# Two-layer mixer and MoE trunk: value block first, weights of the next layer loaded earlier, and half of the first projection ahead of the second tile's norm

## What is computed

```python
z = x @ w_in                                   # 1024 -> 6656 columns: qa ka va ub qc kc vc ga gb gc
merged = sigmoid(ga) * (ya @ w_branch_a) + sigmoid(gb) * (yb @ w_branch_b) + sigmoid(gc) * (yc @ w_branch_c)
x = layer_norm(alpha * x + merged @ w_out, ln1_g, ln1_b)
y = shared_expert(x) + routed_experts(x)       # 64 experts, 8 of them for each token
x = layer_norm(alpha * x + y, ln2_g, ln2_b)    # then the next layer
```

## Time and profile before

| | us |
|---|---|
| median of 3 executions | 1582.39 |
| lowest, highest | 1580.69, 1586.14 |
| the profiled execution | 1581.64 |
| its span | 1579.8 |

### The profile page before, as it was taken

One profiled execution on the slowest core, in us unless ns is written; L12 is line 12 of the kernel. 1 busy time (PEld: TensorE's weight loads), 2 busy tenths in 40 slices (PEclk: granted clock), 3 DMA queues, 4 the chain that ended last, 5 costly groups with the idle time before them and its releaser, 6 DMA issues.

```text
span 1579.8 us, 21900 instructions
## 1 busy us (share of the span) xinstructions
PE 1525.8 (97%) x8898; PEld 948.7 (60%) x8898; DVE 565.5 (36%) x1009; ACT 414.4 (26%) x655; POOL 34.5 (2%) x30
## 2 busy tenths in 40 slices
PE   7999999999999999999789999999999999999996
PEld 7899996444454444445388999864444444544542
DVE  4567735222222222222545577351222222212224
ACT  4545422121111112112235544221111211211111
POOL 0101000000000000000001110000000000000000
PEclk9999999999999999999989999999999999999998
DMA  8543458799999999699733544587999999996991
GB/s 292 175 170 138 153 206 374 288 426 424 415 421 414 405 417 414 244 414 419 282 107 107 187 161 160 210 331 317 426 425 416 419 401 416 419 411 249 415 412 75
DMA packets 79741, 495.86 MB, mean 314 GB/s; under 512 B 6080, under 2 KB 11456, under 8 KB 46656
## 3 DMA queue, kind: packets, MB, share of 16 engines
q1 hardware_dynamic: 77392, 491.31, 76.9%
q10 hardware_dynamic: 2288, 3.67, 0.7%
HBM read 493.92 MB, written 1.05 MB: 313 GB/s over the span
## 4 chain that ended last, share of the span: by engine, by line
PE 94%; DVE 2%; DMA 2%; ACT 1%; issue 1%; SPq 0%; DVEq 0%
PE bank L1406 28%; PE bank L1252 19%; PE bank L1432 14%; PE bank L1361 8%; PE bank L1378 8%; PE bank L1322 4%; PE bank L1209 3%; PE bank L1191 2%; DMA ring_w<-in_w_in 2%; PE bank L1418 1%; PE bank L1393 1%; PE bank L1369 1%; ACT w_hi L594 1%; PE bank L1264 1%; PE bank L1290 1%
## 5 line engine op out<-in xcount | busy, mean ns | idle before, releaser
L1252 PE MATMUL bank<-x_hi,w_hi 128*128 128x256 f32 x688 | 198.4, 288 | 3.5 <-ACT arena L646 1.9
L1252 PE MATMUL bank<-x_lo,w_hi 128*128 128x256 f32 x688 | 195.4, 284 | 0.0
L1252 PE MATMUL bank<-x_hi,w_lo 128*128 128x256 f32 x688 | 195.3, 284 | 0.0
L1126 DVE SCALAR_TENSOR_TENSOR hid<-hid,gate_s,bank 128x256 f32<-128x256 f32 x64 | 30.8, 481 | 399.7 <-ACT hid L707 399.7
L1406 PE MATMUL bank<-arena 128*64 128x512 f32 x768 | 170.1, 595 | 0.0
L1406 PE MATMUL bank<-gu_a,arena 128*64 128x512 f32 x768 | 170.1, 595 | 0.0
L1140 DVE TENSOR_TENSOR y_lo<-bank,y_hi 128x512 fp32r<-128x512 f32 x128 | 88.6, 692 | 225.3 <-ACT y_hi L713 225.3
L777 DVE TENSOR_TENSOR w_lo<-ring_w,w_hi 128x2048 fp32r<-128x2048 f32 x63 | 143.9, 2288 | 66.3 <-ACT w_hi L594 66.2
L1361 PE MATMUL bank<-onehot,xg_hi 128*128 128x256 f32 x512 | 139.9, 306 | 4.0 <-DVE onehot L946 4.0
L713 ACT CAST y_hi<-bank 128x512 fp32r<-128x512 f32 x128 | 74.9, 585 | 246.1 <-PE bank L1432 246.1
L1252 PEld LDWEIGHTS bank<-x_hi,w_hi 128*128 128x128 f32 x688 | 132.7, 193 | 7.5 <-issue 4.0
(11 more groups left out here) (186 smaller groups left out, 1996.4 us busy)
## 6 DMA issues: line engine op xcount, KB each, us to landing
gu_a<-in_expert_w_gate_up SPq DMA_DIRECT2D x24, 4096.0 KB, 13.7
arena<-in_expert_w_gate_up SPq DMA_DIRECT2D x24, 4096.0 KB, 14.6
ring_w<-in_expert_w_gate_up SPq DMA_DIRECT2D x32, 2048.0 KB, 10.9
ring_w<-in_w_in SPq DMA_DIRECT2D x25, 2048.0 KB, 8.6
dn_a<-in_expert_w_down SPq DMA_DIRECT2D x24, 2048.0 KB, 12.1
arena<-in_expert_w_down SPq DMA_DIRECT2D x24, 2048.0 KB, 11.2
dn_c<-in_expert_w_down SPq DMA_DIRECT2D x16, 2048.0 KB, 11.7
ring_w<-in_w_out SPq DMA_DIRECT2D x4, 2048.0 KB, 7.9
```

The source lines that it names most:

```text
L1252: ins = mm(b[:, S * c:S * c + S], lhs, rhs, start=(k == 0 and a + w == 0), stop=(k == KD - 1 and a == 1))
```

## The change

1. The value block `va` is the first of the z blocks, so z tasks 0 and 1 are of the kind that multiplies x (stationary, by token tile) with weights (moving). The attention tasks in `plan()` move by one z task, `rope` of kc stands after z task 10 and `pv` 3 after z task 11.
2. `first_tile(l, u, t)`: z tasks 0 and 1 are done by token tile. In layer 1, PE does the half of tile 0 of z task 0 behind `xt` (0, 1), and that of z task 1 behind `xt` (0, 3); the halves of tile 1 follow as the z tasks. In layer 0 both tiles are done at their task, with the low weights last, and the first low part is cut along k instead of the columns.
3. The second norm of layer 0 is cut in `norm_stats` and `norm_apply`. DVE makes `x_lo` of tile 0 between the statistics and the application of tile 1, and ACT makes `x_hi` of tile 0 ahead of the root of tile 1.
4. SP issues the first two blocks of layer 1 when pair 23 has done its up projection, not after the last expert load.
5. ACT makes the high parts of chunks 0 and 1 behind the SiLU of the last but one pair, that of chunk 2 at the start of the last pair; DVE makes the three low parts between the two pair steps.
6. The low part of z task 19's chunk is made ahead of the reciprocals of `rms` (0, 0).
7. `scores` 0 and 1 each wait for the two z tasks that they read, not for four.

```diff
-Z_BLOCKS = [("qa", 0), ("ka", 512), ("va", 1024), ("qc", 2048), ...
+Z_BLOCKS = [("va", 1024), ("qa", 0), ("ka", 512), ("qc", 2048), ...
-        4: sc(0), 5: sc(1), 6: tr(0) + sc(2), 7: [("pv", 0, 0)] + tr(1) + sc(3),
-        8: [("pv", 1, 0)] + tr(2) + [("rope", 0, 0), ("rope", 0, 1)], 9: [("pv", 2, 0)] + tr(3),
-        10: [("pv", 3, 0), ("rope", 1, 0), ("rope", 1, 1)], 11: sc(4), 12: sc(5), 13: tr(4) + sc(6),
+        5: sc(0), 6: sc(1), 7: tr(0) + sc(2), 8: [("pv", 0, 0)] + tr(1) + sc(3),
+        9: [("pv", 1, 0)] + tr(2) + [("rope", 0, 0), ("rope", 0, 1)],
+        10: [("pv", 2, 0)] + tr(3) + [("rope", 1, 0), ("rope", 1, 1)],
+        11: [("pv", 3, 0)] + sc(4), 12: sc(5), 13: tr(4) + sc(6),
...
-        at[inside[0] if inside else PLAN[last]] = n
+        long = [PLAN[k] for k in range(first, last + 1) if PLAN[k] == ("rms", 0, 0)]
+        at[inside[0] if inside else long[0] if long else PLAN[last]] = n
...
-                for n in range(NB - 2):
+                for n in range(0 if l == 0 else 2, NB - 2):
                     load_block(l, n)
...
+                if l + 1 < L:
+                    sp.wait_ge(up_done, 2 * start + SHORT_FROM - 2)
+                    for n in range(2):
+                        load_block(l + 1, n)
...
-                    if last and l + 1 < L:
-                        for u in range(WBUFS):
-                            split_high(l + 1, u)
+                    if last and odd and l + 1 < L:
+                        split_high(l + 1, 2)
                     act.wait_ge(up_done, n + 1)
                     nc.scalar.activation(hid[:], bank_up[:, 0:FE], ACT.Silu).then_inc(silu_ready, 1)
+                    if last and not odd and l + 1 < L:
+                        split_high(l + 1, 0)
+                        split_high(l + 1, 1)
...
-                for t in range(TT):
-                    norm_std(act, l, 1, t)
+                norm_std(act, l, 1, 0)
+                if l + 1 < L:
+                    for j in range(2):
+                        x_high(l + 1, j)
+                norm_std(act, l, 1, 1)
...
+                    if kind == "rms" and task in LOW_AT:
+                        split_low(l, LOW_AT[task])
...
-                    pair_step(n, u, n - l, last=u == 1)
-                norm(l, 1)
+                    pair_step(n, u, n - l)
+                    if u == 0 and l + 1 < L:
+                        for c in range(WBUFS):
+                            split_low(l + 1, c)
+                norm_stats(l, 1, 0)
+                norm_apply(l, 1, 0)
+                norm_stats(l, 1, 1)
+                if l + 1 < L:
+                    for j in range(2):
+                        x_low(l + 1, j)
+                norm_apply(l, 1, 1)
...
+            def first_tile(l, u, t):
+                n = CHUNK_AT["z", 0, u]
+                tokens = slice(P * t, P * t + P)
+                b = bank(l, ("z", u, 0))
+                pe.wait_ge(w_hi_ready, NC * l + n + 1)
+                for a, w in ((0, 0), (0, 1), (1, 0)) if l else ((0, 0), (1, 0), (0, 1)):
+                    if a:
+                        for g in (2 * t, 2 * t + 1):
+                            wait_evac(pe, l, ("xt", 0, g))
+                    else:
+                        pe.wait_ge(x_hi_ready, 4 * l + 2 * t + 2)
+                    for k in range(KD):
+                        if w and (l, u) == (0, 0) and k == 0:
+                            pe.wait_ge(first_low_ready, 1)
+                        if w and k == (KW if (l, u) == (0, 0) else 0):
+                            pe.wait_ge(w_lo_ready, NC * l + n + 1)
+                        ins = mm(b[:, S * t:S * t + S], (x_hi, x_lo)[a][:, k, tokens], chunk_part((w_hi, w_lo)[w], n)[:, k, :],
+                                 start=(k == 0 and a + w == 0), stop=(k == KD - 1 and (w if l == 0 else a) == 1))
+                return ins
...
+                    elif kind == "z" and i < 2:
+                        for t in range(TT) if l == 0 else (1,):
+                            ins = first_tile(l, i, t)
...
+                    if l and task in (("xt", 0, 1), ("xt", 0, 3)):
+                        u = j // 2
+                        acquire(l, ("z", u, 0))
+                        first_tile(l, u, 0)
```

More of the change, by code:

```diff
@@ L594, in split_high, with x_high @@
                 nc.scalar.copy(chunk_part(w_hi, n), chunk_in(n)).then_inc(w_hi_ready, 1)
+            def x_high(l, j):
+                task = ("xt", 0, j)
+                wait_task(act, l, task)
+                nc.scalar.copy(x_tile(x_hi, j),
+                               bank(l, task)[:].rearrange("p (c n) -> p c n", c=4)).then_inc(x_hi_ready, 1)
             start = 0
@@ L604, in _ @@
                     if kind == "xt" and i == 0:
-                        wait_task(act, l, task)
-                        nc.scalar.copy(x_tile(x_hi, j), b[:].rearrange("p (c n) -> p c n", c=4)).then_inc(x_hi_ready, 1)
+                        if l == 0 or j >= 2:
+                            x_high(l, j)
                         if l == 0 and j == 3:
@@ L729, in _ @@
                 start = start + more * HALVES + HALVES
-                pair_step(2 * start - 2, 0)
+                pair_step(2 * start - 2, 0, last=True)
                 pair_step(2 * start - 1, 1, last=True)
@@ L769, in first_low @@
                 for c in range(2):
-                    cols = slice(P * c, P * c + P)
-                    v.tensor_tensor(lo[:, :, cols], full[:, :, cols], hi[:, :, cols].bitcast(F32),
+                    ks = slice(KW * c, KW * c + KW)
+                    v.tensor_tensor(lo[:, ks, :], full[:, ks, :], hi[:, ks, :].bitcast(F32),
                                     ALU.subtract).then_inc((first_low_ready, w_lo_ready)[c], 1)
@@ L799, in lambdas, with x_low, norm_stats @@
                     step(v.tensor_scalar(nlam[:, l:l + 1], nlam[:, l:l + 1], -lambda_init[l], None, ALU.add))
[L801 to L805, removed]
+            def x_low(l, j):
+                task = ("xt", 0, j)
+                dve.wait_ge(x_hi_ready, 4 * l + j + 1)
+                free(v.tensor_tensor(x_tile(x_lo, j), bank(l, task)[:].rearrange("p (c n) -> p c n", c=4),
+                                     x_tile(x_hi, j).bitcast(F32), ALU.subtract), l, task)
+            def norm_stats(l, which, t):
+                    k = 2 * l + which
                     row = x_tok[:, t, :]
@@ L818, in norm, with norm_apply @@
                     v.bn_aggr(mean_var[:, t, :], stats[:].rearrange("p a b -> p (a b)")).then_inc(var_ready, 1)
+            def norm_apply(l, which, t):
+                    k = 2 * l + which
+                    row = x_tok[:, t, :]
+                    dve.wait_ge(ln_in, 32 * (k + 1))
                     dve.wait_ge(var_ready, TT * k + t + 1)
@@ L960, in _ @@
                     pair = b[:].rearrange("p (c n) -> p c n", c=2)
+                    if kind == "rms" and task in LOW_AT:
+                        split_low(l, LOW_AT[task])
                     if kind == "xt" and i == 0:
-                        dve.wait_ge(x_hi_ready, 4 * l + j + 1)
-                        free(v.tensor_tensor(x_tile(x_lo, j), b[:].rearrange("p (c n) -> p c n", c=4),
-                                             x_tile(x_hi, j).bitcast(F32), ALU.subtract), l, task)
+                        if l == 0 or j >= 2:
+                            x_low(l, j)
                         if (l, j) == (0, 3):
@@ L1081, in _ @@
                                         ALU.subtract).then_inc(y_lo_ready_of[n], 1)
-                    if kind != "scores" and task in LOW_AT:
+                    if kind not in ("scores", "rms") and task in LOW_AT:
                         split_low(l, LOW_AT[task])
@@ L1090, in _ @@
                     if task == ("branch", 2, 3):
-                        norm(l, 0)
+                        for t in range(TT):
+                            norm_stats(l, 0, t)
+                            norm_apply(l, 0, t)
                     if task == ("router", 0, 0):
@@ L1103, in _, with pair_step @@
                         later_rounds(l)
-                def pair_step(n, odd, combined_before, following=None, last=False):
+                def pair_step(n, odd, combined_before, following=None):
                     bank_up, bank_other = (bank_even, bank_odd)[::-1 if odd else 1]
@@ L1222, in _ @@
                             ins = nc.tensor.transpose(b[:, P * c:P * c + P], x_tok[:, t, 4 * (j % 2) + c::KD], ident)
+                    elif kind == "z" and i < 2:
+                        for t in range(TT) if l == 0 else (1,):
+                            ins = first_tile(l, i, t)
                     elif kind == "z":
-                        if i == 0:
-                            for g in range(4):
-                                wait_evac(pe, l, ("xt", 0, g))
                         n = CHUNK_AT["z", i // 2, i % 2]
                         hi, lo = chunk_part(w_hi, n), chunk_part(w_lo, n)
[L1229 to L1240, removed]
```

(6 more changed lines are left out.)

7 lines of the change are left out of this document (1 added, 6 removed).

## The result

The changed kernel takes 1568.84 us (median of 4 executions, 1567.74 to 1570.28) beside 1582.98 us for the kernel before: a ratio of 0.9912, 95% interval 0.9900 to 0.9924. It was run twice more with the kernel before beside it, and gave 0.9921 (0.9908 to 0.9935) and 0.9919 (0.9906 to 0.9933). The forecast was 1572.9 us with a range of 1569.5 to 1578.5. The median of all 14 executions of the changed kernel is 1569.4 us, at the range's lower end.

A forecast was written before the change was run, and what follows sets the result against it. PE, busy 97% of the span, was taken as the bound; gains of 1.6 + 4.6 + 3.3 = 9.5 us took the profiled 1581.64 to 1572.1, plus 0.75 for the median: 1572.9 us, range 1569.5 to 1578.5.

The forecast's parts named there:

- Last pair: Last pair of layer 0: with blocks loaded early, the product starts sooner after the up projection; gain 1.6 us, bounds 1.0 and 2.1.
- Transfer: Expert stage, pair 23: two weight blocks fit a hole in DMA, in by 664 us; price 0, at worst 10.8 us.
- Between the layers: From the second norm to z task 1 of layer 1: early half tiles gain 4.6 us, bounds 1.4 and 5.8.
- The price on the second norm: Between the layers: making two `x_lo` first delays the second tile's `ln_done` by 1.2 us.
- Low part ahead of the reciprocals: Mixer, ahead of `branch` (1, 0): the wait goes, gain 1.9 us in each layer before the new task order's price.
- The price for the new order of tasks: Mixer, after z task 10: the second `rope` may wait; 0.25 us a layer taken, 0.7 at most.
- the first step: Whole kernel: PE is busy 97% of the span, so time can come only from its gaps or low-clock matmuls.
- The estimate by the Trainium skill: Low clock between the layers: throttled time times share taken away gives 2.8 us more, sum 12.3; not used in the forecast.
- B: Between the layers or mixer: the clock or a new wait takes most of a term, 1576.1 or 1576.2 us; chance 0.22.
- C: Between the layers: no slow matmul, gain 5.8 us; with other terms at their bounds 11.7, time 1570.7 us; chance 0.08.
- D: Expert stage: the 4.2 MB load does not fit the hole at pair 23; slower, 1583.7 to 1588.4 us; chance 0.04.
- E: Half tiles do not start early and the mixer's new wait eats its gain; 1578.5 to 1581 us; chance 0.04.

The follow-up runs named there:

- the filled pair: The kernel before and the changed kernel, each with matmuls on constants put in PE's idle places: medians 1575.97 and 1567.13 us.
- the filled kernel: The changed kernel with matmuls on constants into free banks in four idle places of PE: ratio to the kernel before 0.9900, median 1567.13 us.

## Why the prediction was right and wrong

**Last pair: right.** 1.6 us in the sum, 1.8 in the profile. The fit of ACT's two casts into 3.98 us held, and DVE is what is late now, as said. What the step left out is that behind PE's stop of 2.1 us there the clock fell in three of four profiles: it is the place at 774.

**Transfer: right**, price 0, in by 662 for a forecast of 664.

**Between the layers: right in mechanism, 0.6 us short.** 4.6 forecast, 5.2 in the profile. 14 matmuls of the half tile started at half clock and not 18, 0.4 us; the other 0.2 is in the time before, where the sum ended z task 1 at 810.6 and the profile at 810.84. The second turning ran at the full clock (0.90 us), as the sum took it. The price on the second norm was 1.0 us, forecast 1.2. The sum took the early halves as the whole gain; the run without them has 1.4 of it. There z tasks by token tile do not wait for the last `x_lo`, and fewer of their matmuls meet the low clock.

**Low part ahead of the reciprocals: right.** 3.8 us forecast before its price, gaps of 1.88 from start to start gone in both layers, alone, and back when it was taken back. The price for the new order of tasks, forecast at 0.25 us a layer at the second `rope` of z task 10, was 0.25 as idle time of PE and 0.4 from start to start. The mixer of layer 1 gained 1.6 us, forecast 1.65.

**What failed** is the first step: "So time can come only from PE's gaps, or from matmuls at a low clock; the change removes no matmul." The sentence names the low clock, and the working then looked for it between the layers alone. Everywhere else it was taken that a stretch that is not edited stays as long as it is. The kernel before had two low stretches at the gathering, 1.7 us each, that a table by stretch would have shown, and a third place at 774 in which it may fall. None of the sum's terms holds them, and the changed kernel has lost them and has one at 74 instead. Why the falls went there no run shows; taking part 6 alone back brought the one at 283 again. The balance in the two profiles is 3.4 - 1.6 = 1.8 us. Over all executions the filled pair puts the clock's part at 4 us, of which the sum had about 1 (the second turning at the full clock). The bounds were made from the terms, and had no room for it. A second, smaller step failed beside it: 0.75 us were added to get from the profiled execution to the median. The profiled execution of the changed kernel came out 12.4 us lower and not 9.5, and its median lies 0.4 us below it, not 0.75 above: 2.9 and 1.2 us of the 4.1 by which the forecast was too high. That 0.75 was the difference of three executions from one, and the spread of the executions (1567.7 to 1570.3 in the changed kernel) is larger than it.

The estimate by the Trainium skill, "TensorE: Matmul & The Clock Gate", section Terms (throttled time multiplied by the share taken away), gave 12.3 us in the sum, which happens to be the span's difference. It is no support: the rule put all of the surplus between the layers, where 5.2 us were gained, and the runs show it elsewhere. By the profiles the low stretch between the layers is 13.7 us long before and 6.8 after; the rule gives 3.4 us for the difference, while the faster turning (1.0) and four slow matmuls fewer (0.4) make 1.4. For the short stretches at the gathering, in which PE is busy nearly throughout, rule and trace do agree: 3.4 us at half speed cost 1.7.

**The rivals.** B did not come: no term was eaten. C (no slow matmul at all) did not come by itself either; the filled kernel shows it, at 1567.1 and not 1570.7, since it fills more places. D, the slower side, had the empty stretch at 656 against it, and the blocks were in by 662. E did not come: the half tile starts 3.35 us after the first turning did, 3.5 in the sum.

## What to carry to other kernels

Before a sum of saved gaps is made, list every stretch of the whole span in which the granted clock is low, and what PE did ahead of each; a change can win or lose some 1.7 us at each of them without touching it, here 4 us on top of 9. Where two kernels are to be compared in the order of their work alone, fill PE's short idle places in both with small matmuls on constants into a bank that is free: it separates the two causes, and here it was a gain of its own (6.2 and 2.2 us). When a dependent product can be cut by token tile, look at the cut even if no half can be started early: here it alone removed the wait of 1.6 us for the last tile's evacuation.

## What the runs showed of the hardware that was not expected

Behind stops of PE of 1.9 to 2.2 us (at 280, 774 and 1065 us) the clock fell for 3.4 us in three of four profiles each, and in one and the same profile it fell behind one such stop and not behind another (282 and 774 us). In the kernels of the new order the stops ahead of the gathering are as long (2.0 and 1.9 us), and where they were not filled the clock fell behind one of twelve, in six profiles. So the order of the work went with the clock at a place that no edit touched; by what, no run shows. And a place with two stops of 0.95 and 0.98 us, nine microseconds apart, with a z task and small matmuls between them, had a fall in layer 0 in all seven profiles of the new order and in none of five of the old, though the tasks around it are the same. In layer 1 of all twelve the same stops had none. Why it is steady at this one place was not settled. Filling only the second of the two stops, with 12 matmuls, was enough to keep the clock. The filling cost nothing that can be seen: the 32 matmuls fit into a stop of 2.0 us and left 0.25 of it.
